# Keys and values of a cached page by separate transfers, in the ring of a paged block-sparse attention

## What is computed

```python
k_full = cache_k[page_table[:, :c * ppb]].reshape(DB, c, MOBA_BLOCK, H, Dh)
kmean = jnp.mean(k_full, axis=2)
gate = jnp.einsum('bthd,bjhd->bhtj', qf, kmean)
_, sel = lax.top_k(gate, n_sel)
...
probs = jax.nn.softmax(jnp.concatenate([lp for lp, _, _ in parts], axis=-1) * scale, axis=-1)
...
    out = out + jnp.einsum(spec, pr, vals.astype(f32))
```

## Time and profile before

| what | value |
|---|---|
| median of three runs | 1301.92 us (1301.61 to 1302.52) |
| profiled execution, its own time | 1303.04 us |
| span of its trace | 1301.3 us |
| granted clock of PE, mean | 0.98 |
| PE busy | 1207.9 us, 93% of the span |
| DVE, ACT, POOL busy | 618.0, 413.9, 434.4 us |
| read from HBM | 207.78 MB |

### The profile page before, as it was taken

How to read it: one execution, slowest core, us unless ns; L and a number is a source line. 1 busy time by engine, 2 the same in 40 slices (tenths; PEclk the granted TensorE clock), 3 DMA queues, 4 the chain that set the end, 5 groups by cost and what they waited for, 6 DMA issues and landing times. The chain is left out here.

```text
span 1301.3 us, 33258 instructions
## 1 busy us (share of the span) xinstructions
PE 1207.9 (93%) x14362; PEld 1099.4 (84%) x14362; DVE 618.0 (47%) x1071; ACT 413.9 (32%) x773; POOL 434.4 (33%) x299
## 2 busy tenths in 40 slices
PE   6999998988899899887889999989999999999994
PEld 6998997766666667655689999989999999999994
DVE  6457896444555555674562222244444444440003
ACT  5142331333333333323522222333333333342110
POOL 3333453011101111010143333635555555564440
PEclk9999998999999999999899999989999999999998
DMA  5222215988798889789622222312222222222211
GB/s 212 98 102 66 80 53 227 388 332 326 274 378 318 296 329 376 269 291 378 227 81 82 82 82 82 114 44 82 82 82 82 82 82 83 96 88 88 90 58 73
DMA packets 57251, 216.28 MB, mean 166 GB/s; under 512 B 6609, under 2 KB 6994, under 8 KB 56338
## 3 DMA queue, kind: packets, MB, share of 16 engines
q1 hardware_dynamic: 57106, 214.17, 45.8%
HBM read 207.78 MB, written 6.37 MB: 165 GB/s over the span
## 5 line engine op out<-in xcount | busy, mean ns | idle before, releaser
L667 PE MATMUL ps<-buffer_at 128*128 128x288 f32 (+2 forms) x5760 | 778.4, 297 | 6.5 <-POOL buffer_at L1549 6.5
L667 PEld LDWEIGHTS ps<-buffer_at 128*128 128x128 f32 x5760 | 772.7, 190 | 13.0 <-POOL buffer_at L1549 7.2
L1549 POOL TENSOR_TENSOR buffer_at<-buffer_at 128x1024 fp32r<-128x1024 f32 (+1 forms) x118 | 331.8, 2814 | 340.1 <-ACT buffer_at L1254 339.5
L1254 ACT ACTIVATE buffer_at<-buffer_at 128x1024 fp32r<-128x1024 f32 (+1 forms) x118 | 129.2, 1097 | 287.6 <-PE ps L667 134.5
L1601 POOL TENSOR_TENSOR buffer_at<-buffer_at 128x256 f32<-128x256 f32 x45 | 40.4, 928 | 324.6 <-DVE buffer_at L1844 324.6
L1520 ACT ACTIVATE buffer_at<-buffer_at 128x592 f32<-128x592 f32 x44 | 38.9, 884 | 161.8 <-DVE buffer_at L2233 158.6
L2231 DVE TENSOR_TENSOR buffer_at<-ps,buffer_at 128x512 f32<-128x512 f32 x44 | 30.4, 692 | 125.6 <-PE ps L667 125.5
L1052 PE MATMUL ps<-buffer_at 128*32 128x128 f32 x2048 | 73.7, 283 | 15.5 <-ACT buffer_at L1375 8.7
L1944 DVE TENSOR_REDUCE buffer_at<-ps 128x1 f32<-128x256 f32 (+1 forms) x68 | 28.0, 412 | 103.2 <-PE ps L1019 103.1
L1019 PE MATMUL ps<-buffer_at 128*32 128x256 f32 x1024 | 72.6, 399 | 4.2 <-DMA buffer_at<-in_kvcache 2.9
L1052 PEld LDWEIGHTS ps<-buffer_at 128*32 128x32 f32 x2048 | 54.4, 112 | 25.0 <-issue 11.5
(11 more groups left out here) (247 smaller groups left out, 1280.1 us busy)
## 6 DMA issues: line engine op xcount, KB each, us to landing
buffer_at<-in_kvcache SPq DMA_DIRECT2D x256, 512.0 KB, 6.0
buffer_at<-in_w_up SPq DMA_DIRECT2D x44, 512.0 KB, 3.5
buffer_at<-in_w_in SPq DMA_DIRECT2D x42, 512.0 KB, 3.5
buffer_at<-in_w_down SPq DMA_DIRECT2D x16, 704.0 KB, 4.1
buffer_at<-in_w_br SPq DMA_DIRECT2D x8, 512.0 KB, 3.5
buffer_at<-in_w_o SPq DMA_DIRECT2D x8, 512.0 KB, 3.5
buffer_at<-in_xin SPq DMA_DIRECT2D x4, 576.0 KB, 7.0
buffer_at<-in_xin SPq DMA_DIRECT2D x1, 2304.0 KB, 10.5
```

The source lines that it names most:

```text
L667: ins = e.matmul(out, lhs, rhs[:, cols], start=(start and i == 0), stop=(stop and i == 2))
L1254: e.activation(hi[:, :, :], raw, ACT.Copy).then_inc(w_hi, 1)
L1549: e.tensor_tensor(lo[:, :, :], raw, hi[:, :, :], ALU.subtract).then_inc(w_lo, 1)
```

## The change

A page is moved by two transfers, one for its 512 columns of keys and one for its 512 columns of values, in rows of 2 KB. For each fill SP first issues the four key parts, as soon as the logits of fill f-3 are done, then the four value parts, as soon as its value product is done. Each buffer has two semaphores: `k_fill`, for which the key product waits, and `vw_fill`, for which the value product waits. `vw_fill` is shared with the weights of the last product, whose waits count from the number that the values leave behind (`in_slot`).

```diff
--- before.py
+++ after.py
@@ -500,9 +500,10 @@
 
 
         s_c0, s_c1, s_pv, s_s0 = (sem(n) for n in ("ones_in", "const_in", "params_in", "states_in"))
+        in_slot = [64 * sum(slot_of(f) == i for f in range(FILLS)) for i in range(4)]
         s_x = sems("x_in", 4)
-        kv_fill = sems("kv_fill", RING)
-        w_a, w_g, w_u, w_d = sems("w_in", 4), sems("w_gate", 3), sems("w_up", 4), sems("w_down", 4)
+        k_fill = sems("k_fill", RING)
+        w_a, w_g, w_u, vw_fill = sems("w_in", 4), sems("w_gate", 3), sems("w_up", 4), sems("v_fill_w_down", 4)
         w_hi, w_lo, xh_ready, xs_even, xs_odd, hh_hi, hh_lo, yb_split, oa_split, st_stored = (sem(n) for n in (
             "w_hi", "w_lo", "xn_hi", "xn_lo_even", "xn_lo_odd", "hh_hi", "hh_lo", "yb_split", "oa_split", "state_stored"))
         oa_hi = sem("oa_hi")
@@ -578,14 +579,16 @@
                 found = [nc.values_load_multi_w_load_instructions(
                     ptab[0:1, (2 * p + s) * NPG + 2 * j:(2 * p + s) * NPG + 2 * j + 2], engines=(mybir.EngineType.SP,),
                     min_val=0, max_val=kvcache.shape[0] - 1)[1] for s in range(2)]
-                if f >= RING:
-                    e.wait_ge(sa_pv, fill_step(f - RING) + 1)
-                elif f == 0:
+                if f == 0:
                     e.wait_ge(p_tile, NR + NQ)
-                for s in range(2):
-                    for a, pg in enumerate(found[s]):
-                        e.dma_start(kvring[slot_of(f)][:, 2 * s + a, :],
-                                    kvcache[bass.ds(pg, 1)].rearrange("o p n -> p (o n)")).then_inc(kv_fill[slot_of(f)], 16)
+                for part, filled in ((0, k_fill), (1, vw_fill)):
+                    if f >= RING:
+                        e.wait_ge((sa_lg, sa_pv)[part], fill_step(f - RING) + 1)
+                    cols = slice(part * WA, (part + 1) * WA)
+                    for s in range(2):
+                        for a, pg in enumerate(found[s]):
+                            e.dma_start(kvring[slot_of(f)][:, 2 * s + a, cols],
+                                        kvcache[bass.ds(pg, 1)].rearrange("o p n -> p (o n)")[:, cols]).then_inc(filled[slot_of(f)], 16)
 
             for f in range(FILLS):
                 if f == STATES_IN:
@@ -645,7 +648,7 @@
                     e.wait_ge(up_mm, 2 * NF - 3 + i)
                 elif i >= 4:
                     e.wait_ge(dn_mm, i - 3)
-                e.dma_start(wd[i % 4], w_down[c][:, h * KH:(h + 1) * KH, :]).then_inc(w_d[i % 4], 16)
+                e.dma_start(wd[i % 4], w_down[c][:, h * KH:(h + 1) * KH, :]).then_inc(vw_fill[i % 4], 16)
             e.wait_ge(up_cp, 2 * NF)
             e.dma_start(conv_out, cvo[:, :, :]).then_inc(stored, 16)
             for i in range(4):
@@ -1013,7 +1016,7 @@
                                           start=(s == 0), stop=(s == 1))
                 else:
                     f = step_fill(i)
-                    e.wait_ge(kv_fill[slot_of(f)], 64 * nth_fill(f))
+                    e.wait_ge(k_fill[slot_of(f)], 64 * nth_fill(f))
                     for s in range(2):
                         for hp in range(HP):
                             m_ = e.matmul(ps[32 * hp:32 * hp + 32, 7, 0:BLK], qbd[:, (2 * p + s) * HP + hp, :],
@@ -1047,6 +1050,7 @@
                                           vsm[0:NS, hp * P:(hp + 1) * P], start=(s == 0), stop=(s == 1))
                 else:
                     f = step_fill(i)
+                    e.wait_ge(vw_fill[slot_of(f)], 64 * nth_fill(f))
                     for k in range(4):
                         for hp in range(HP):
                             m_ = e.matmul(ps[32 * hp:32 * hp + 32, 6, 0:P], pT[i % 2][:, k, 32 * hp:32 * hp + 32],
@@ -1522,7 +1526,7 @@
                 if n < 2 * NF:
                     w_split(wuh[n % 2], wr[n % 4], w_u[n % 4], 16 * (n // 4 + 1))
                 else:
-                    w_split(wdh[n - 2 * NF], wd[n - 2 * NF], w_d[n - 2 * NF], 16)
+                    w_split(wdh[n - 2 * NF], wd[n - 2 * NF], vw_fill[n - 2 * NF], in_slot[n - 2 * NF] + 16)
                 if q % 2:
                     e.wait_ge(up_cv, q + 1)
                     e.activation(cc[s], cc[s], ACT.Silu).then_inc(up_si, 1)
@@ -1533,7 +1537,7 @@
                 hh_split(j)
             for i in range(2, 2 * KT + 4):
                 if i < 2 * KT:
-                    w_split(wdh[i % 4], wd[i % 4], w_d[i % 4], 16 * (i // 4 + 1))
+                    w_split(wdh[i % 4], wd[i % 4], vw_fill[i % 4], in_slot[i % 4] + 16 * (i // 4 + 1))
                 if i >= 4 and HALVES[i - 4][1]:
                     c = HALVES[i - 4][0]
                     e.wait_ge(y_done, c + 1)
```

## The result

The changed kernel takes 1323.0 us (median of four runs, 1321.41 to 1326.7) beside 1302.22 us for the kernel before (four runs, 1301.61 to 1304.36). The ratio is 1.0154 with a 95% interval of 1.0134 to 1.0174: slower by 20.8 us, where 8.5 were forecast. The direction was right; the size was wrong, and 1323.0 lies outside the stated range of 1303 to 1320.

The account below looks back on a forecast made before the run. SP's issuing was taken to bound the loop: 6.7 us a fill plus 4.85 us until keys land made fill 47 late by 8.5 us, nothing elsewhere. Added to the 1301.92 us median this gave 1310.4 us, range 1303 to 1320.

Parts of the forecast that it names:

- SP's line: In the loop, key issue of fill f begins at 207.7 + 0.5 + 6.7 f us, SP never waiting; fill 47 late by 8.5.
- SP's time a fill: In the loop, eight transfers for four raise SP's cost from 4.14 us to 6.43 to 6.73 with stalls; 6.7 taken.
- the landing: At the key product, three issues (1.55 us) plus 3.3 us until the fourth key page lands: 4.85; landing bounds 2.5 and 6.0.
- SP as the bound: In the loop, SP's issuing sets the pace and makes keys late: +8.5 us, 1310.4 us in all; chance 0.76.
- SP's waits, PE's waits and their place at the key product: Signs in the loop: SP's waits fall from 135 to under 20 us, PE's page waits exceed 10, all at the key product.
- The stalls: Slow issues on SP just after instruction fetches: 0.21 us a fill before, growing to 0.5 with eight transfers.
- the DMA engines would have idle time: In the loop's dense windows, 2 KB rows take the engines 5.7 us a fill, below SP's 6.7; share below 0.9.
- my own list: Signs against the forecast, among them DMA share staying at 0.95 with fills 7 us apart, which would mean packets.
- The clock: In the loop, PE waiting for keys may lose some clock; nothing added, range widened by 2 us.
- The early request: In the loop, keys requested after the logits gain at most 2.9 us of PE's waits; the new waits show next to nothing.
- the rival with 1299.0 us: In the loop, SP's extra time stays hidden and earlier keys end 2.9 us of PE's waits; chance 0.06.
- No visible change: In the loop, stalls do not grow, SP takes 6.43 us a fill: 1303.3 us; chance 0.14.

Follow-up runs that it names:

- experiment 3: Changed kernel with one load of four page numbers per fill instead of two of two, without bounds checks: 1299.75 us, 0.9959 times the kernel before.
- experiment 8: Changed kernel with one load of four page numbers per fill instead of two of two, bounds checks kept: 1304.76 us, 0.9994 times the kernel before.
- 4: Kernel before, whole pages in four transfers, with three more unused loads of page numbers on SP in each fill: 1334.12 us, 1.0228 times before.
- 5: Changed kernel with keys waiting for the value product three blocks back, as values do: 1325.29 us, 1.0156 times the kernel before.
- 7: Changed kernel with one unchecked load of four page numbers, and keys waiting for the value product as values do: 1299.83 us, 0.9945 times before.
- experiment 1: Kernel before with each page moved by two transfers of 64 partitions, rows still 4 KB: 1439.79 us, 1.1029 times before.
- experiment 2: Kernel before with keys and values apart in the buffer: four transfers a fill, each row two runs of 2 KB; 1307.72 us, 1.0036 times before.

## Why the prediction was right in direction and wrong in size

Two terms of the sum failed: SP's line, which reaches fill 47 8.4 us later than forecast, above all through SP's time a fill, and the landing, which takes 3.9 us longer. The mechanism, SP as the bound, held; that the DMA engines would have idle time, which the landing rested on, did not.

**SP as the bound: right, and shown.** Taking work from SP (3, 8) gives the time back with the packets unchanged; adding work to SP alone (4) takes it with the packets of before. SP's waits, PE's waits and their place at the key product came as forecast.

**SP's time a fill: 6.7 taken, 6.86 measured.** The kernel before has 4.39, so the sum of 4.14 and a stall of 0.21 was nearly sound. The stalls grew a little more than taken: over 43 fills the issues took 25.0 us above their median of 0.33 (10.5 us before), 0.58 us a fill for the 0.5. That makes 4.14 + 2.08 + 0.58 = 6.80; the last 0.06 I did not trace. Over 43 fills 0.16 us is 6.9 us. With fill 3 already 0.9 us behind the line and the states' load at 1.49 us instead of 0.5 (the trace before already had 1.29 us for this issue), fill 47 begins at 532.02 instead of the 523.6 of the line: +8.4 us. The step as written was "between 6.43 us (stalls do not grow) and 6.73 us": too narrow above, on a term that counts 43 times. The range went to 6.9 us a fill, so this term alone would have stayed inside it. One reading behind the stalls was off as well: of the 22 slow issues 21, not all, began less than 0.75 us after a fetch had started; the other began 1.51 us after.

**The landing: 4.85 us taken, 7.5 to 8.7 measured.** From the first key issue to the key product went 7.52 us at fill 13, 8.13 at fill 26 and 8.71 at fill 47, all with PE waiting. I built the fourth landing, 3.3 us, from single transfers on quiet engines. The upper bound beside it, 6.0, the median of queued pages, gives 1.55 + 6.0 = 7.55 and would have been right at fill 13. I assumed that a late SP leaves the engines nearly empty. It does not: the windows of those two waits, fill 13 and fill 47,

```profile
296.91:304.43 7.52, 5.05 (x119) 3.77 (x120) 1.65 (x4) 1.61 (x5) 0.00 (x0) 1.00 0.97 319
...
532.02:540.73 8.71, 6.89 (x195) 5.68 (x188) 5.68 (x11) 1.50 (x5) 4.42 (x5) 1.00 1.04 403
```

move 319 x 7.52 = 2.40 MB and 403 x 8.71 = 3.51 MB, where the four key parts are 1.05 MB. At fill 13 the rest are the values of the fill before, issued just ahead of the keys, and the values of the same fill, issued behind them. At fill 47 another 1.05 MB are the states, whose load, issued at 528.30, landed 9.6 us later, in the middle of this window; the forecast counted 0.5 us of SP's time for it and nothing on the engines. The keys share the engines with all of these. How much of the 2.7 to 3.9 us belongs to each was not tried; values on another queue, or issued later, would tell.

Together at step 50: 8.5 forecast, 8.4 by the later line and 3.9 by the landing give the 20.8 us by which that key product is late. Either error alone would have left the forecast time inside the range (1318.8 and 1314.3 us); both together did not. That the medians of the two kernels also differ by 20.8 us is chance, since the profiled executions differ by 18.4. After fill 47 the loop regained 2.8 us up to its last key product (20.8 to 18.0); I had counted 8.7 of slack there, but none of it in the sum.

**DMA engines: the share was read wrongly.** I forecast a share below 0.9; it was 0.98, 0.91 and 0.98. By my own list a share of 0.95 with fills 7 us apart would have meant packets, and the profile alone seemed to say so. Experiments 3 and 8 refute it: the same packets flow at 382 GB/s with a share of 1.04. The 5.7 us a fill that I took for the engines stands beside 2.1 MB at 382 GB/s, 5.5 us. A high share here does not mean that the engines set the pace.

**The clock.** The profiled execution of the change lost no clock to PE's waits in the loop: 0.99 from 218 to 650 us, against 0.98 before. Its three other runs have a mean of 0.975 to 0.978 over the program instead of 0.981 and took 1.2 to 5.3 us longer; no trace shows in which stage.

**The early request.** The gain was put at no more than 2.9 us, and the wait for the logits was to show nothing: right, and experiments 5 and 7 show that it is worth nothing with a late or a light SP. The split is worth something once SP is fast enough, which I had not forecast (the rival with 1299.0 us gave this number, but by the early request).

**The rivals.** "No visible change" needed 6.43 us a fill; experiment 8, at 6.10, shows that world. The Trainium skill, DMA: Bandwidth & Descriptors, section Issuing engines are not separate DMA queues, holds the sequencer's time to be usually small beside the transfer. The runs disagree here: 0.76 us of SP's time a fill, with the transfers unchanged, is 18 us of the kernel.

## What to carry to other kernels

Before splitting a transfer, add up the issuing engine's own time per round, loads of addresses, checks and stalls with it, and compare it with the pace of the loop: below it the split cost nothing here (experiments 3, 7 and 8), above it the excess counts once per round. Where it comes close, first make that queue's other work cheaper; one load for two was worth 18 us here. And take the landing of a piece from queued transfers, not from a lone one, even where the issuer is late.

## What the runs showed of the hardware that was not expected

- Transfers of 64 of 128 partitions flowed at 232 GB/s with the engines' share at 0.98, against 387 for whole pages, and took 0.47 us to issue instead of 0.33 (experiment 1). One of two runs a row (128 x 2 x 512) took 0.54 us (experiment 2).
- The DMA share is no measure of spare room: 0.98 at 331 GB/s in the change, 1.04 at 382 with the same packets (experiment 3), 0.99 at 387 with larger ones before.
- The load of four page numbers in one costs SP no more than 0.30 us, where each load of two took 0.47, in the rows of the loads:

```profile
L579 SPq TENSOR_LOAD <-ptab x128: 467/474/1712, 181.5 to 649.1; - x128
...
L579 SPq TENSOR_LOAD <-ptab x64: 294/298/522, 181.4 to 624.6; - x64
```

  The first row is the change's, the second that of experiment 8.
- Of the 61 issues of the change that took over 0.1 us longer than their median, 41 ended 0.36 to 0.37 us after an instruction fetch (16 KB, queue q8) ended on one of the DMA engines. That is a coincidence in time seen in the trace, in the same way before (21 of 24) and after; no run here moved the fetches, so its cause stays open.
